# Attention logits from split q and k: three rounded-format products per tile in a TensorE-bound encoder layer

## What is computed

```
proj = rmsnorm(x) @ w_in                  # u, z_ssm | q, k, v, z_att, f_logit
q = rmsnorm_per_head(q); k = rmsnorm_per_head(k)     # 8 heads of 128
logit[t, s] = q_t . k_s / sqrt(128) + (c_t - c_s)    # s <= t, c = cumulative log-forget sums
p = softmax(logit);  o = p @ v
y_att = rmsnorm(o * silu(z_att))
x = x + concat(y_ssm, y_att) @ w_out      # y_ssm comes from the S5 state-space branch
```

## Time and profile before

| | |
|---|---|
| median of 3 runs | 2005.78 us (2004.67 to 2006.36) |
| profiled execution, first to last instruction (its span) | 2005.4 us |
| TensorE busy | 1961.9 us, 98% of the span |
| VectorE, ScalarE, GpSimd busy | 51%, 33%, 22% |
| granted TensorE clock, mean over the span | 0.995 |
| one head's 32 slots | 121.2 us |

### The profile page before, as it was taken

How to read it: one execution, slowest core, us unless ns; L and a number is a source line. 1 busy time by engine, 2 the same in 40 slices (tenths; PEclk the granted TensorE clock), 3 DMA queues, 4 the chain that set the end, 5 groups by cost and what they waited for, 6 DMA issues and landing times.

```text
span 2005.4 us, 35481 instructions
## 1 busy us (share of the span) xinstructions
PE 1961.9 (98%) x12368; PEld 1901.1 (95%) x12368; DVE 1017.3 (51%) x1985; ACT 657.0 (33%) x1336; POOL 449.2 (22%) x716
## 2 busy tenths in 40 slices
PE   5999999999999999999999999999999999999999
PEld 4899999999999999999999999999989999999998
DVE  7765566555453544635445354554656643333333
ACT  6432233333433333343333433343454431111110
POOL 5865444455110010010100101010010112222221
PEclk8999999999999999999999999999999999999999
DMA  8343434435322121131211212121274623333332
GB/s 227 103 119 101 110 108 107 108 103 133 86 54 63 35 83 36 34 85 31 85 34 45 74 34 82 35 66 52 72 264 136 217 77 87 86 89 87 86 86 66
DMA packets 220264, 179.91 MB, mean 90 GB/s; under 512 B 33090, under 2 KB 200156, under 8 KB 218996
## 3 DMA queue, kind: packets, MB, share of 16 engines
q1 hardware_dynamic: 202336, 126.31, 23.5%
q0 software_dynamic: 12352, 41.79, 6.9%
q10 hardware_dynamic: 5524, 11.14, 1.5%
HBM read 133.24 MB, written 45.93 MB: 89 GB/s over the span
## 4 chain that ended last, share of the span: by engine, by line
PE 89%; DVE 5%; issue 2%; DMA 1%; POOL 1%; ACT 1%; SPq 0%; DVEq 0%; POOLq 0%; ACTq 0%
PE GB L187 65%; PE TB L187 9%; PE TB L1957 3%; PE TB L1978 3%; PE TB L1999 2%; PE TB L1139 1%; PE TB L1140 1%; PE TB L1129 1%; PE TB L2018 1%; PE TB L2058 1%; DVE XL L668 1%; PE TB L1943 0%; DMA out_k_sample<-KO 0%; DMA xt<-in_x_prompt 0%; PE TB L1033 0%
## 5 line engine op out<-in xcount | busy, mean ns | idle before, releaser
L187 PE MATMUL GB<-XH,whi 128*128 128x384 f32 x2832 | 956.6, 338 | 7.2 <-DVE UP L744 5.5
L187 PE MATMUL GB<-XH,wlo 128*128 128x384 f32 x2832 | 927.5, 327 | 0.0
L187 PE MATMUL GB<-XL,whi 128*128 128x384 f32 x2832 | 924.7, 327 | 0.0
L175 DVE TENSOR_TENSOR wlo<-wraw,whi 128x256 fp32r<-128x256 f32 x540 | 271.6, 506 | 701.3 <-ACT whi L171 697.3
L187 PEld LDWEIGHTS GB<-XH,whi 128*128 128x128 f32 x2832 | 533.0, 188 | 22.6 <-issue 9.5
L187 PEld LDWEIGHTS GB<-XL,whi 128*128 128x128 f32 x2832 | 533.3, 188 | 5.3 <-issue 3.8
L171 ACT CAST whi<-wraw 128x256 fp32r<-128x256 f32 x540 | 218.3, 406 | 960.7 <-PE GB L187 799.5
L187 PEld LDWEIGHTS GB<-XH,wlo 128*128 128x128 f32 x2832 | 532.4, 188 | 0.0
L1358 POOL DMA_DIRECT2D ya_s<-ZR x7 | 4.1, 586 | 729.6 <-DVE ZR L1716 729.6
L1763 DVE RECIPROCAL SQ<-SQ 128x136 f32<-128x136 f32 x128 | 127.6, 997 | 1.1
L187 PE MATMUL TB<-XH,wlo 128*128 128x384 f32 (+1 forms) x384 | 125.8, 328 | 0.0
(11 more groups left out here) (388 smaller groups left out, 2032.2 us busy)
## 6 DMA issues: line engine op xcount, KB each, us to landing
wraw<-in_w_in SPq DMA_DIRECT2D x380, 128.0 KB, 2.2
wraw<-in_w_out SPq DMA_DIRECT2D x128, 128.0 KB, 2.1
xt<-in_x_prompt SPq DMA_DIRECT2D x5, 1024.0 KB, 5.8
NCB<-nc_s POOLq DMA_DIRECT2D x8, 608.0 KB, 5.1
us_s<-UP SPq DMA_DIRECT2D x8, 548.0 KB, 2.9
U<-us_s SPq DMA_DIRECT2D x64, 68.5 KB, 3.0
vs_s<-SS SPq DMA_DIRECT2D x8, 548.0 KB, 2.7
YT<-vs_s SPq DMA_DIRECT2D x64, 68.5 KB, 2.8
```

What stands on the lines that cost most here:

```text
L175: V.tensor_tensor(wlo[:, s % SPL], wraw[:, s % RAW], whi[:, s % SPL].bitcast(f32), ALU.subtract).then_inc(self.lo, 1)
L187: ins = T.matmul(group(GB if bank is None else bank, b), w[:, s % SPL, kk], x[:, k + kk, c:c + n], start=first and kk == 0 and i == 0, sto ...
```

## The change

1. QR is split by GpSimd into QH (rounded, float32r) and QL (QR less QH). KR is normalised in place, and split in the same way into KH and KL. The tiles QN and KN are gone. "qn" now follows QL, and "kl" follows KL. The split of k stands in GpSimd's list behind the loads and ahead of the stores.
2. Each logits tile is three float32r products, QH by KH, QH by KL, QL by KH, in the place of one float32 product. The first row waits for "kl" where it waited for "kn".
3. The cached keys are split too: ACT writes KPH, DVE writes KPL at s = 5 (behind that slot's row). The sample block's logits and the transposes behind s = 5 wait for "kpl".
4. `onesr` is one column, read 128 times over by the sums of squares.

```diff
-            onesr = sbp("onesr", [P, P], r32)
-            QN, KN = sbp("QN", [P, TOK]), sbp("KN", [P, TOK])
+            onesr = sbp("onesr", [P, 1], r32)
+            QH, QL, KH, KL = (sbp(n, [P, TOK], r32) for n in ("QH", "QL", "KH", "KL"))
...
             # GpSimd, part()
-                        G.tensor_copy(QN[:], QR[:]).then_inc(e["qn"], 1)
+                        G.tensor_copy(QH[:], QR[:]).then_inc(e["qh"], 1)
+                        pool.wait_ge(e["qh"], h + 1)
+                        stand(pool, "pool")
+                        G.tensor_tensor(QL[:], QR[:], QH[:].bitcast(f32), ALU.subtract).then_inc(e["qn"], 1)
...
                         pool.dma_start(NCB[:], nc_s[ds(h, 1), :].to_broadcast([P, CT])).then_inc(e["in"], 16)
+                        pool.wait_ge(e["kn"], h + 1)
+                        stand(pool, "pool")
+                        G.tensor_copy(KH[:], KR[:]).then_inc(e["kh"], 1)
+                        pool.wait_ge(e["kh"], h + 1)
+                        stand(pool, "pool")
+                        G.tensor_tensor(KL[:], KR[:], KH[:].bitcast(f32), ALU.subtract).then_inc(e["kl"], 1)
...
             # ScalarE and VectorE
-                            S.copy(KPT[:], TB[:, 1024:1024 + PAST]).then_inc(e["kpt"], 1)
+                            S.copy(KPH[:], TB[:, 1024:1024 + PAST]).then_inc(e["kpt"], 1)
+                        if att and s == KPT_AT:
+                            dve.wait_ge(e["kpt"], ha + 1)
+                            V.tensor_tensor(KPL[:], TB[:, 1024:1024 + PAST], KPH[:].bitcast(f32), ALU.subtract).then_inc(e["kpl"], 1)
...
-                            V.scalar_tensor_tensor(KN[:], KR[:], vec[:, 33:34], SQ[:], ALU.mult, ALU.mult).then_inc(e["kn"], 1)
+                            V.scalar_tensor_tensor(KR[:], KR[:], vec[:, 33:34], SQ[:], ALU.mult, ALU.mult).then_inc(e["kn"], 1)
...
             # TensorE
-                                T.matmul(TB[:, d:d + n], onesr[:], SQH[:, c:c + n], start=True, stop=False)
+                                T.matmul(TB[:, d:d + n], onesr[:].to_broadcast([P, P]), SQH[:, c:c + n], start=True, stop=False)
...
-                                pe.wait_ge(e["kn"], ha + 1)
+                                pe.wait_ge(e["kl"], ha + 1)
...
+                            def logits(out, c, kh, kl, r):
+                                T.matmul(out, QH[:, c:c + r], kh, start=True, stop=False)
+                                T.matmul(out, QH[:, c:c + r], kl, start=False, stop=False)
+                                return T.matmul(out, QL[:, c:c + r], kh, start=False, stop=True)
...
-                                    ins = T.matmul(TB[:, c:c + cw], q, KN[:, c:c + cw], start=True, stop=True)
+                                    ins = logits(TB[:, c:c + cw], i * P, KH[:, c:c + cw], KL[:, c:c + cw], P)
...
-    nc = _bacc.Bacc("TRN2", target_bir_lowering=False, num_devices=1)
+    nc = _bacc.Bacc("TRN2", target_bir_lowering=False, num_devices=1, dynamic_dma_scratch_size=8192)
```

More of the change, by code:

```diff
@@ L1170, in attention @@
             PT = sbp("PT", [P, SEQ])
-            CK, CV, KPT = sbp("CK", [PAST, P]), sbp("CV", [PAST, P]), sbp("KPT", [P, PAST])
+            with ExitStack() as over:
+                CK = over.enter_context(nc.sbuf_tensor("CK", [PAST, P], f32))
+            KPH, CV, KPL = sbp("KPH", [P, PAST], r32), sbp("CV", [PAST, P]), sbp("KPL", [P, PAST], r32)
             qg, bf = sbp("qg", [P, 1]), sbp("bf", [NH, 1])
@@ L1176, in attention @@
             NR = 9
-            fx, fl, fe, one8, cum0, cum1, lfs = (KN[0:NH], ZR[0:NH], NCB[0:NH, 0:TOK], QN[0:NH, 0:SEQ], PR[0:NH], PT[0:NH, 0:PAST + DEC],
+            flat8 = lambda a: a[0:NH].rearrange("p m d -> p (m d)")
+            fx, fl, fe, one8, cum0, cum1, lfs = (flat8(KO)[:, 0:TOK], ZR[0:NH], NCB[0:NH, 0:TOK], flat8(VT)[:, 0:SEQ], PR[0:NH], PT[0:NH, 0:PAST + DEC],
                                                  PT[0:NH, 512:512 + PAST + DEC])
-            cl, lt = CK[:, 0:NH], KPT[:, 0:TT * NH].rearrange("p (m h) -> p m h", h=NH)
-            names = ("ga", "gd", "sq", "ss_mm", "rt", "qn_r", "qn", "kn", "kpt_mm", "kpt", "s_mm", "nmx", "exp", "pn",
+            cl, lt = CK[:, 0:NH], DM[:, 0:TT * NH].rearrange("p (m h) -> p m h", h=NH)
+            names = ("ga", "gd", "sq", "ss_mm", "rt", "qn_r", "qh", "qn", "kn", "kh", "kl", "kpt_mm", "kpt", "kpl", "s_mm", "nmx", "exp", "pn",
                      "pt_mm", "pt_act", "pt_dve", "o_mm", "y", "v_mm", "v_act", "v_dve", "k_mm", "k_act", "k_dve",
@@ L1493, in part @@
                                 act.wait_ge(e["qn"], h)
+                            if s == 15 and att:
+                                act.wait_ge(e["kl"], h)
                             act.wait_ge(W.done[0], W.tiles + 4 * h + s // 8 + 1)
@@ L1513, in part @@
                                     state_space_over(act)
-                                    S.copy(onesr[:], ones[:].to_broadcast([P, P])).then_inc(e["or"], 1)
+                                    S.copy(onesr[:], ones[:]).then_inc(e["or"], 1)
                             if not att and s == 8:
@@ L1693, in part @@
                                 dve.wait_ge(e["qn"], h)
+                            if s == 15 and att:
+                                dve.wait_ge(e["kl"], h)
                             V.tensor_copy(cols(raw, 1), group(GB, 1)).then_inc(e["gd"], 1)
@@ L1939, in part @@
                             for c, d, n in parts:
-                                T.matmul(TB[:, d:d + n], onesr[:], SQH[:, c:c + n], start=True, stop=False)
+                                T.matmul(TB[:, d:d + n], onesr[:].to_broadcast([P, P]), SQH[:, c:c + n], start=True, stop=False)
                             pe.wait_ge(e["sql"], 2 * h + w + 1)
                             for c, d, n in parts:
-                                ins = T.matmul(TB[:, d:d + n], onesr[:], SQL[:, c:c + n], start=False, stop=True)
+                                ins = T.matmul(TB[:, d:d + n], onesr[:].to_broadcast([P, P]), SQL[:, c:c + n], start=False, stop=True)
                             ins.then_inc(e["ss_mm"], 1)
@@ L1973, in part @@
                                 pe.wait_ge(e["nmx"], NR * ha + p)
+                            def logits(out, c, kh, kl, r):
+                                T.matmul(out, QH[:, c:c + r], kh, start=True, stop=False)
+                                T.matmul(out, QH[:, c:c + r], kl, start=False, stop=False)
+                                return T.matmul(out, QL[:, c:c + r], kh, start=False, stop=True)
                             if i < NR - 1:
-                                q = QN[:, i * P:(i + 1) * P]
                                 for c in range(0, w, 512):
                                     cw = min(512, w - c)
-                                    ins = T.matmul(TB[:, c:c + cw], q, KN[:, c:c + cw], start=True, stop=True)
+                                    ins = logits(TB[:, c:c + cw], i * P, KH[:, c:c + cw], KL[:, c:c + cw], P)
                             else:
[L1980 to L1983, removed]
+                                pe.wait_ge(e["kpl"], ha + 1)
+                                logits(TB[0:DEC, 0:PAST], SEQ, KPH[:], KPL[:], DEC)
+                                ins = logits(TB[0:DEC, PAST:w], SEQ, KH[:, SEQ:TOK], KL[:, SEQ:TOK], DEC)
                             ins.then_inc(e["s_mm"], 1)
@@ L1993, in part @@
                             if s > KPT_AT:
-                                pe.wait_ge(e["kpt"], ha + 1)
+                                pe.wait_ge(e["kpl"], ha + 1)
                             if p:
@@ L2005, in part @@
                         if gemm and s in (KT_AT, VT_AT):
-                            src, base, name = (KN, 0, "k") if s == KT_AT else (VR, 1024, "v")
+                            src, base, name = (KR, 0, "k") if s == KT_AT else (VR, 1024, "v")
                             if s == KT_AT:
```

## The result

| | before | changed |
|---|---|---|
| median of 4 runs each, us | 2005.22 (2004.46 to 2006.36) | 2039.83 (2039.38 to 2041.68) |
| ratio, 95% interval | | 1.0172 (1.0158 to 1.0186) |
| span of the profiled execution, us | 2005.4 | 2038.7 |
| granted clock, mean | 0.995 | 0.986 |

What follows compares the result with a forecast made beforehand. TensorE, busy 98%, was taken as the bound. Products -9.4, stalls +24.2, clock falls +10.5 and the rest +1 summed to +26.3 us on 2005.8: 2032 us, slower by 1.3%, range 2018 to 2052.

Steps and rivals of the forecast that it cites:

- products: TensorE's logits: three float32r products cheaper than one float32, 1.17 us a head, -9.4 us over 8 heads.
- seven stalls for KL: TensorE's first logits row waits for KL on GpSimd: 3.4 us in six heads, 3.8 in head 7, +24.2 us.
- clock falls behind them: TensorE's clock falls once behind each of the seven stalls, some 1.5 us each: +10.5 us, bounds 0 and 21.
- KPL and the rest: TensorE's transposes wait 0.1 to 0.3 us a head for KPL, +1 us; loads, stores and `onesr` cost nothing.
- head 0: First head's first logits row: no addition, GpSimd's list early, KL ends long before; no stall, 0 us.
- behind head 7: Forecast had no term here; it used TensorE's 2.99 us idle up to 1498.11 only to price a clock fall.
- the middle of the bounds: Products' sum: -12 if short ones cost only their columns, -6 if their whole record; -9.4 taken.
- its rivals: At the stall: conversions dear at 2.54 us each, 2052 to 2062 us, 12%; KL in time, 1996 to 2001, 6%.
- the 0.4 that the row of wlo allowed: Head 1, GpSimd: if VectorE's wlo from 747.03 comes first, KL ends at 750.0 in place of 749.6.
- The bound of two falls for each: Upper bound of the clock term: two clock falls behind each stall, 21 us in place of 10.5.

Runs made afterwards that it cites:

- kernel 5: Also written early_spaced: the early-split order of kernel 1, with QH held until VectorE has both SQL of that head; 2000.04 us, ratio 0.9974.
- 7: Kernel 5 with one float32 product of QH and KH per logits tile, QL and KL made but left out; 2009.47 us, ratio 1.0023.
- kernel 1: Changed kernel with only GpSimd's list reordered, both splits ahead of the square addition; 2005.25 us, ratio 0.9998.
- casts_early: Changed kernel with both conversions, QH and KH, moved ahead of the square addition, subtractions left in place; 2011.06 us, ratio 1.0029.
- float32_logits: Changed kernel with one float32 product of QH and KH per logits tile, QL and KL made and waited for; 2044.56 us, ratio 1.0198.
- keys_out_first: Kernel 5 with the store of k issued ahead of the store of v in every head; 1998.57 us, ratio 0.9966.

## Why the prediction was right, and where it was not

| term | forecast, us | found, us |
|---|---|---|
| products | -9.4 | -9.4 (kernels 5 and 7) |
| seven stalls for KL | +24.2 | +24.1 listed idle, +25.2 start to start |
| clock falls behind them | +10.5 | about +17 |
| KPL and the rest | +1 | +1 to +1.6 |
| head 0 | 0 | +3.7 |
| behind head 7 | 0 | -3.7 |
| sum | +26.3 | about +34 (span +33.3, medians +34.6) |

**The products: right,** in sum and in form. A short tile costs by its weights' loads and a long one by its columns, and the middle of the bounds was the value.

**The stall: right in place, number, releaser and size,** and its rivals fall. The conversions cost 1.10 us and the subtractions 2.53 to 2.54, as the rows of a copy and of a two-input operation said. KL was not in time. Two small things cancel: the gap ahead of the conversion is 0.60, not 0.28, and KL was lengthened by 0.2 and not by up to the 0.4 that the row of wlo allowed. Head 7 is 4.4 and not 3.8, and the 3.8 itself has the semaphore's 0.28 once too often: by the steps of head 1 its list ends at 1477.7, which gives 3.5.

**The clock falls: the term that was mis-sized.** The step said "I count one fall for each", with the price of 1.5 us from the one fall that the trace of before could be read for. The first stall was like that: 3.4 us at 0.5, about 1.6 us lost. Behind the six others the clock stays at 0.5 for 6.8 us, which costs 2.65 each over the idle, and about 2 in head 7, where 2.3 us of it lie in the idle. 1.6 + 5 x 2.65 + 2 = about 17. The bound of two falls for each, 21, held the value; the point taken didn't. The stretch at 1499 could have told only of the short form.

**Head 0: missed.** The step said "Head 0 has no addition and its list is early, so KL ends long before its first row: none". That is true of KL, but I looked only at the end of the list. Its new first part, QL, now meets VectorE's SQ and SQL, and the engines block each other: SQL takes 3.39 us for 1.29, QL 3.64 for 2.54. TensorE waits for that SQL 3.17 us in place of 1.06 (+2.1) and the clock falls behind it (+1.6):

```profile
589.70:593.10 3.40, 3.40 (x12) 3.40 (x12) 0.00 (x0) 2.63 (x4) 0.00 (x0) 0.50 0.70 222
```

The cause is shown by kernel 5, which only spaces the two and gets 5.2 us back over kernel 1. I had weighed the Trainium skill's rule that a VectorE operation with two SBUF inputs and a GpSimd one that reads SBUF exclude each other (SBUF — State Buffer, "Who interferes with whom") at one wlo, for 0.2 us a head, and nowhere else. The lines of head 0 agree with it, one operation ending 2.34 and the next 1.15 us behind the one before, and there it was worth 3.7.

**Behind head 7: missed, and it paid.** The wait of 2.99 us shrank to 0.76 (-2.2) and its fall didn't come (-1.5). This is no saving of the change, but an effect of the fall behind head 7's stall. Counted from the first row of head 7 (1474.13 before, 1510.23 now), VectorE is ready for its multiply after 13.3 us before and 15.5 now, with TensorE's pieces at 0.5 for 4.5 us behind the row (in casts_early and early_spaced, with no fall there, it is 13.5); and KO's load landed after 15.8 before and 14.3 now. The first of the two goes with the fall; why the load was sooner stays open. The stall alone gives nothing: casts_early has 2.85 us of it at head 7 and no fall, and its wait is 5.4. In kernel 1, which has neither, the wait is 4.1. That this gain cancels head 0 is luck; without it the sum would have been off by 3.7 more. As it is, most of the error is the clock's term.

What stays open is what sets the length of a fall. It isn't the idle's length alone: float32_logits has the idles of the changed kernel and falls of half the length in five of the seven heads. What the traces show is that it goes with the place where the fall begins. Over the ten kernels' traces, between the start-up and the end, there are 35 falls behind idles of TensorE. The 14 long ones, 6.8 us, begin 0.45 to 2.3 us ahead of the first product behind the idle (1.1 in the lines at 877.55); the 21 short ones, 3.4 us, begin at most 0.36 ahead of it or behind it (1.3 behind in head 1). Nor does the program fix whether a fall comes: the idles of 1.0 and 1.6 us up to 549 are the same in all ten, and seven traces have a short fall there, two a long one and one, casts_early's, none.

## What to carry to other kernels

When work is added to an in-order engine that no stage waits for, look where in its list it stands and what that list waits for: here the same instructions cost 35 us behind one late wait, nothing ahead of it, and gained 5 once they were also kept apart from VectorE's. Price such a stall with the clock that may fall behind it, and take the longest form of a fall for the upper bound. And look for the second engine that each moved two-input operation now runs beside, in every head, the first and the last too.

## What the runs showed of the hardware that I had not expected

- After the same TensorE idle of 3.33 us the clock stood at 0.5 for 3.4 us in one kernel and 6.8 in another, and in the changed kernel itself for 3.4 in head 1 and 6.8 in heads 2 to 5. Idles of 1.45 us and, beside casts_early's first rows, 1.12 us brought none. Near 3 us it can go either way: casts_early's 2.85 us brought none, keys_out_first's 2.83 a fall of 3.4 us. A fall of 6.8 us cost 2.65 us beyond its idle, since part of it lay in the idle.
- A VectorE operation of 0.42 us took 3.51: it started while GpSimd issued DMAs, 0.67 before the subtraction behind them, and ended after that subtraction. The issue by itself does not do this. In the ten traces some 220 of these operations (wlo) lie beside an issue with no GpSimd operation right behind it, and all took 0.41 to 0.43 us; so did the ten beside an issue with a fill right behind. The 15 that took longer, 0.67 to 3.52, all had the conversion KH or the subtraction KL right behind the issues; one more with KL there took 0.42. Why VectorE is held before that operation is listed as started stays open.
- A GpSimd subtraction suffers as well: 3.64 us for 2.54 when it starts beside a VectorE multiplication (SQ) of 1088 columns.
- GpSimd writes float32r at the speed of float32: a conversion of 128 x 1088 in 1.10 us where the copy took 1.09.
